# Leaving out TensorE products that nothing reads, ahead of the experts and before the last sum

## The reference

```python
mixed = concat([stick_breaking(q, k, v), cross_attention(qc, mem)]) @ w_out
h = h + rms_norm(mixed, attn_post_g)

xn = rms_norm(h, ffn_pre_g)
logits = xn @ w_router                      # 256 x 8
top_vals, top_idx = lax.top_k(logits, 2)
gates = softmax(top_vals), put at top_idx
for e in range(8):                          # 1024 -> 3584 -> 1024
    y = (silu(xn @ w_gate[e]) * (xn @ w_up[e])) @ w_down[e]
    out = out + gates[:, e:e+1] * y
h = h + rms_norm(out, ffn_post_g)
```

## Time and profile before

| | us |
|---|---|
| median of 3 runs | 1377.7 (1377.0 to 1378.1) |
| the profiled execution's own time | 1376.42 |
| its span | 1374.5 |
| PE busy | 1358.1 |
| DVE busy | 370.2 |
| ACT busy | 285.8 |
| granted clock, mean over the span | 0.996 |

### The profile page before, as it was taken

One profiled execution on the slowest core, in us unless ns is written; L12 is line 12 of the kernel. 1 busy time (PEld: TensorE's weight loads), 2 busy tenths in 40 slices (PEclk: granted clock), 3 DMA queues, 4 the chain that ended last, 5 costly groups with the idle time before them and its releaser, 6 DMA issues.

```text
span 1374.5 us, 25953 instructions
## 1 busy us (share of the span) xinstructions
PE 1358.1 (99%) x11499; PEld 690.8 (50%) x11499; DVE 370.2 (27%) x432; ACT 285.8 (21%) x381; POOL 90.3 (7%) x226
## 2 busy tenths in 40 slices
PE   9999999999999999999999999999999999999997
PEld 7956888888889853333333333333333333333332
DVE  5765544555565421101101101001010110110111
ACT  5455344444466530010000000000001001001001
POOL 3002000000100062010010000001001001000000
PEclk9999999999999999999999999999999999999998
DMA  8807655555363399999999999999999999999982
GB/s 261 280 29 279 223 186 184 184 184 184 120 218 112 114 409 335 421 414 420 421 417 420 420 416 419 421 417 419 420 418 418 421 419 417 421 419 416 420 362 80
DMA packets 96076, 445.14 MB, mean 324 GB/s; under 512 B 9570, under 2 KB 20002, under 8 KB 63460
## 3 DMA queue, kind: packets, MB, share of 16 engines
q1 hardware_dynamic: 92032, 431.56, 79.6%
q0 software_dynamic: 3936, 11.98, 2.6%
q10 hardware_dynamic: 4, 0.01, 0.0%
HBM read 436.53 MB, written 6.98 MB: 323 GB/s over the span
## 4 chain that ended last, share of the span: by engine, by line
PE 96%; DVE 2%; ACT 1%; issue 0%; DMA 0%; POOL 0%; DVEq 0%; ACTq 0%
PE psum L1112 42%; PE psum L1127 14%; PE psum L539 8%; PE psum L541 8%; PE psum L540 8%; PE psum L1131 7%; PE psum L662 2%; PE psum L498 1%; PE psum L521 1%; PE psum L851 1%; PE psum L528 1%; PE psum L842 1%; PE psum L775 0%; PE psum L909 0%; DVE reg_a L1635 0%
## 5 line engine op out<-in xcount | busy, mean ns | idle before, releaser
L1112 PE MATMUL psum<-ring,reg_a 128*32 128x384 f32 (+1 forms) x6144 | 578.8, 539 | 0.0
L1112 PEld LDWEIGHTS psum<-ring,reg_a 128*32 128x32 f32 x6144 | 199.6, 110 | 377.1 <-issue 377.0
L1996 DVE TENSOR_TENSOR work<-memb,psum 128x1152 f32<-128x1152 f32 (+1 forms) x16 | 40.0, 2500 | 517.5 <-PE psum L1112 517.5
L539 PE MATMUL psum<-w_hi,x_hi 128*128 128x512 f32 (+2 forms) x320 | 122.2, 382 | 0.5 <-DVE x_lo L1661 0.2
L1127 PE MATMUL psum<-ring,reg_b 128*32 128x512 f32 x1024 | 121.6, 592 | 0.0
L541 PE MATMUL psum<-w_hi,x_lo 128*128 128x512 f32 (+2 forms) x320 | 120.5, 376 | 0.0
L540 PE MATMUL psum<-w_lo,x_hi 128*128 128x512 f32 (+2 forms) x320 | 120.3, 376 | 0.0
L1666 DVE TENSOR_TENSOR w_lo<-raw,w_hi 128x2048 fp32r<-128x2048 f32 x42 | 96.1, 2290 | 81.9 <-ACT w_hi L1270 81.9
L1510 ACT ACTIVATE memb<-psum 128x1152 f32<-128x1152 f32 (+1 forms) x16 | 20.7, 1291 | 385.4 <-PE psum L1112 385.4
L1270 ACT ACTIVATE w_hi<-raw 128x2048 fp32r<-128x2048 f32 x42 | 80.4, 1917 | 94.0 <-PE psum L541 94.0
L1127 PE MATMUL psum<-ring,reg_a 128*32 128x512 f32 x768 | 91.2, 592 | 0.0
(11 more groups left out here) (298 smaller groups left out, 1145.6 us busy)
## 6 DMA issues: line engine op xcount, KB each, us to landing
ring<-in_l_w_down SPq DMA_DIRECT2D x112, 1024.0 KB, 20.3
ring<-in_l_w_gate SPq DMA_DIRECT2D x64, 1024.0 KB, 20.4
ring<-in_l_w_up SPq DMA_DIRECT2D x64, 1024.0 KB, 20.3
ring<-in_l_w_gate SPq DMA_DIRECT2D x64, 768.0 KB, 18.8
ring<-in_l_w_up SPq DMA_DIRECT2D x64, 768.0 KB, 19.3
raw<-in_l_w_gate SPq DMA_DIRECT2D x14, 1024.0 KB, 5.2
raw<-in_l_w_up SPq DMA_DIRECT2D x14, 1024.0 KB, 5.2
raw<-in_l_w_down SPq DMA_DIRECT2D x14, 1024.0 KB, 5.2
```

Of the source, the lines that this page charges most:

```text
L539: pe.matmul(out, x[0], w[0], start=first, stop=False, skip_group_check=True)
L1112: ins = pe.matmul(psum[G * c:G * c + G, b0 + g, 0:w], picked[:, g, k, :], x[:, w * c:w * c + w], start=(k == 0), stop=(k == KD - 1), skip_ ...
L1996: dve.tensor_tensor(x.rearrange("p (g c r) -> p g c r", g=NGRP, r=G), act_e[:, 0:NGRP * w].rearrange("p (g r c) -> p g c r", g=NGRP, r=G), ...
```

## The change

All products that nothing reads are taken out: `keep_running` with its six calls (18 products) and the one product at line 1162. `keep_running` also held a wait for bank 1 to be drained, which goes with it; the waits of all other instructions stay, and no other instruction moves.

```diff
             mix_late(1)
-            def keep_running(n):
-
-                pe.wait_ge(drained[1], bk.count[1])
-                for _ in range(n):
-                    pe.matmul(bank(1), h_hi[:, 0, 0:P], h_hi[:, 1, :],
-                              start=True, stop=True, skip_group_check=True)
-
-            keep_running(2)
             pe.wait_ge(small_in, 16 * 3)
...
             turn(FPRE1, "f1T", (2, 3), [0])
-            keep_running(5)
             router_rows(0, 2)
-            keep_running(3)
             for hf in range(2):
...
                 end(ins, label)
-            keep_running(1)
             router_rows(1, 0)
-            keep_running(4)
             pe.wait_ge(chosen_ok, 1)
             begin(("rank",), 5)
...
             end(ins, ("rank",))
-            keep_running(3)
             pe.wait_ge(rows_ok, NT)
             pe.wait_ge(pick_ok, 1)
...
                 pe.wait_ge(pickT_ok, 1)
-                pe.matmul(bank(1), ident[:, :], hid_e[:, 0:512], start=True, stop=True, skip_group_check=True)
                 pe.wait_ge(below_ok, NT)
```

## The result

| | before | after |
|---|---|---|
| median of 20 runs, us | 1377.94 (1376.67 to 1379.12) | 1379.76 (1376.93 to 1382.18) |
| profiled execution, us | 1376.42 | 1382.10 |
| its span, us | 1374.5 | 1380.1 |
| mean granted clock | 0.996 | 0.993 |

The ratio of after to before is 1.0012, with a 95% interval of 1.0006 to 1.0017. The 20 times of after stand in three groups: nine from 1376.9 to 1378.2, nine from 1379.7 to 1380.5, and two at 1382.1 and 1382.2. The median falls just at the foot of the middle group: with nine executions in the first group and eleven above it, two more cheap ones would have put it near 1378. The means differ by 1.45 us (twice the standard error is 0.76). The profiled execution is one of the last two, so its 5.7 us are not the change's usual price, and part of them is not the change's at all. I go through them in order.

The account below looks back on a forecast made before the run. PE was taken as the bound, with no idle time in the experts. Terms 0 - 0.1 + 3.0 + 0.2 = +3.1 us on 1376.42 gave 1379.5, plus 1.3 for the median 1380.8; range 1377.8 to 1383.6.

Parts of the forecast that it names:

- my main case: Clock falls at the pre-gather and rises late, at 497.0 us: 1380.2 to 1382.6 us, chance 0.46.
- the quick rise: Rival: clock falls at the pre-gather but is back at 494.5 us: 1379.6 us, chance 0.30.
- The 18 products hold nothing up: 0.: Before the pre-gather: what follows the keep_running products waits for DVE or ACT, so removing them gains 0.
- The end's product holds up `own` by 0.1.: At line 1162: `own` waits for `h_hi` until about 1360.8 us, so removal gains 0 to 0.1, taken as 0.1.
- A fall at 490.8.: In the pre-gather: clock drops 4.0 us after thin work begins at 486.8 us; bounds 489 and no fall.
- The rival of no fall: Thin stretch before the pre-gather is too short for the clock to drop: 1377.6 us, chance 0.13.
- the rival of an early fall by 484: Clock drops in the stretch thinned by the first ten products, slowing the second `router_rows`: about +4.8, 1382.5 us, chance 0.09.
- the 2.8 us that the prediction sets against a limit on idle gaps: Between second `router_rows` and pre-gather: 2.8 us nearly empty; the skill warns only of longer idle gaps, so clock would just hold.
- The price of the fall, 3.0 us.: Pre-gather loses 2.4 us at the lower clock and the first experts 0.6; ends 1.1 and 5.3 us.
- The 3.7 us of work that the prediction puts before a rise: From the program's start, 9.14 to 12.8 us: back-to-back work of about 3.7 us was enough to raise the clock.
- The end: 0.2.: In `own`: without line 1162's product the clock may fall sooner, costing 0 to 1.0 us, taken as 0.2.
- The other side,: Rival: removed products do delay what follows; 2.3 us and line 1162's 0.9 come off: 1374.5 us, chance 0.02.

Follow-up runs that it names:

- after_again: The changed kernel run again, 11 runs beside the kernel before: mean span +1.14 +- 0.61 us, ratio 0.9998 to 1.0016.
- look_4a: One more profiled execution of the changed kernel, nothing further changed: 1381.0 us.
- look_4b: Another profiled execution of the changed kernel, nothing further changed: 1379.04 us.
- narrow: Kernel before with all 18 keep_running products writing 8 columns instead of 512, line 1162 kept: mean span +1.37 +- 0.78 us, ratio 1.0002 to 1.0021.
- eighteen_only: Kernel before without the 18 keep_running products, line 1162 kept: mean span +0.49 +- 0.35 us, ratio 0.9993 to 1.0011.
- early_eleven: Kernel before without the last two keep_running calls (7 products), first four calls and line 1162 kept: mean span +0.98 +- 0.56 us, ratio 0.9998 to 1.0016.
- end_only: Kernel before without the product at line 1162, all 18 keep_running products kept: mean span +0.07 +- 0.19 us, ratio 0.9993 to 1.0011.
- seven_no_end_4: Kernel before with only the last seven keep_running products, line 1162 also out: mean span +0.15 +- 0.20 us, ratio 0.9991 to 1.0009.

## Why the prediction was right

I forecast +3.1 us, 1380.8, with a range of 1377.8 to 1383.6; measured are +1.8 us by the medians, 1379.76. The way and the cause were right, the size was too large, and my chances leaned a little to slower by over 0.2% where it is 0.12%. That the number came this close is in part luck. It lies outside the 1380.2 to 1382.6 of my main case and next to the 1379.6 of the quick rise, but no single case of mine was measured: the median stands at the edge between two groups, and on the chip of after_again the same kernel was only 0.46 us above by the medians.

- *The 18 products hold nothing up: 0.* Right. Every load waits for the same releaser as before. I missed that they cost ACT's row copies 0.2 us (4.36 against 4.16), so the pre-gather now starts 0.2 us sooner after the projection.
- *The end's product holds up `own` by 0.1.* It is 0: 1.94 us from the last down products to `own` with it and without it.
- *A fall at 490.8.* It came between 489.4 and 490.6 in all four profiled executions of the changed kernel. The rival of no fall is out for these; for the executions of the fastest group of the 20 it is not shown either way. None of PE's idle times there was longer than 1.29 us: the 2.8 us that the prediction sets against a limit on idle gaps are broken by the rank products, and the clock fell all the same. Of the rival of an early fall by 484 there is no trace: the second `router_rows` takes 2.02 us as before. The Trainium skill's rule on transposes ("TensorE: Matmul & The Clock Gate", Part 4), by which it would have come, is not borne out.
- *The price of the fall, 3.0 us.* The pace was right (0.228 us a record by the earlier trace rows; 1.91 times as long). The length was mis-sized: I put the rise at 497.0. It is 496.2 in two of the four and 493.4 and 494.0 in the other two, which is the rival of the quick rise, so the term is 2.75 or 1.63 us and not 3.0. In none of the four do the experts lose anything, since the clock is back while the pre-gather still runs. The 3.7 us of work that the prediction puts before a rise were one case, too: in the profiled execution of after, the same work started at 9.18 and the clock was up only near 14.8 us (L521's 16 records take 4.76 us in place of 3.78, about 2 us more at the lower level).
- *The end: 0.2.* This is the other term that I mis-sized, in the other direction: +1.50, +1.06, +1.19 and -0.33 in the four (in the order after, look_4a, look_4b, after_again). I had priced an early fall there at 1.0 and taken a fifth of it.
- *The other side,* 2.3 us of products on the chain that come off: wrong, and narrow shows it once more, where their work comes off and it is slower. The chain put 14.6% down to instructions that delayed nothing.

Two terms that were off partly cancelled: 0.3 to 1.4 us too much in the middle, 0.9 to 1.3 too little at the end where it fell early. With the 0.2 us of ACT, the parts of the change add up to 4.05, 3.6, 2.6 and 1.1 us in the four profiled executions, around my 3.1. The median is lower because it is over executions of which, by their times, nine of 20 had a cheap kind.

## What to carry to other kernels

Products that nothing reads can be worth their place where PE would otherwise have little to do ahead of work that it must do at full pace; they delay nothing as long as what follows them waits for another engine, which is read at its weight load and not in the chain, and they can still slow another engine a little (0.2 us here). Put them into the last empty stretch ahead of the dense work: here seven did what nineteen did. Price a fall from the same instruction at both levels, and take its length from several executions, since one profile shows only one of the cases.

## What was not expected of the hardware

The low stretches in the middle had two lengths only, 3.4 and 6.8 us, in eight profiled executions. What differed in the chip between executions of one kernel was when the clock rose at the start (by the pace of L521, later than 13 us in some), which moves everything after it by up to 1.2 us.

The two ends of the program seem to be tied together. The clock's fall in `own` came 3.7 us after the first `own` product before the change, and 1.6, 2.2 and 2.1 us after it in three executions of the changed kernel; with the seven products in place, or with the end's product in place, never sooner than 3.7. What the end's product does shows where a profile with it and one without it have a fall in the middle and `own` at nearly the same distance from the clock's rise after it. The kernel of eighteen_only differs from the changed kernel in that product alone. In look_4b `own` starts 868.3 us after that rise and the clock falls 870.4 us after it; in eighteen_only `own` starts 868.5 us after it, and the fall comes at 873.8, when PE is done, as these stretches of eighteen_only show:

```profile
1362.20:1367.40 5.20, 4.55 (x13) 1.99 (x12) 1.34 (x2) 1.24 (x2) 0.00 (x0) 1.00 0.00 0
1367.50:1372.00 4.50, 0.00 (x0) 0.00 (x0) 4.16 (x4) 1.18 (x4) 1.51 (x4) 0.50 0.19 78
```

The profiled execution of after and that of early_eleven, which keeps the product, both start `own` 868.8 us after the rise, and the falls come at 870.4 and 877.2. These are single executions. That it takes the fall in the middle to bring the end to where the product matters fits all the profiles too, but only two of them have neither that fall nor the product (end_only and seven_no_end_4), and both had a late rise at the start, so it stays open.

ACT's two row copies take 4.15 to 4.17 us where the last two calls are out or have 8 columns, 4.24 with the last three products, and 4.30 to 4.37 with seven or eleven; why, the traces don't show.
